# Placing SBUF buffers at multiples of 2048 and 128 bytes in a fused two-block transformer kernel

## The reference, cut to what matters

```python
# first block, for each of 2 layers
h = rmsnorm(x, norm_mix[l])
q, k, v, u, ug, ga, gb = split(h @ w_in[l])
a_out = sliding_window_attention(rope(rmsnorm(q)), rope(rmsnorm(k)), v, sinks[l])
c_out = silu(layernorm(depthwise_conv(u * sigmoid(ug)))) @ w_conv_out[l]
x = x + (sigmoid(ga) * a_out + sigmoid(gb) * c_out) @ w_out[l]
g, up = split(rmsnorm(x, norm_ffn[l]) @ w_gate_up[l])
x = x + (silu(g) * up) @ w_down[l]                    # d_ff = 2816
# second block, 1 layer
mod = silu(c) @ w_ada + b_ada
x = x + g1 * (concat(ssd_mixer(h), stick_breaking_mixer(h)) @ w_out)
x = x + g2 * ((silu(h @ w_gate) * (h @ w_up)) @ w_down)
```

## The kernel before

| buffers | before: byte | rest by 128 | rest by 2048 |
|---|---|---|---|
| x | 16,512 | 0 | 128 |
| hh, hl | 32,896, 49,280 | 0 | 128 |
| raw, wh, wl | 65,664, 73,856, 90,240 | 0 | 128 |
| tmp | 106,624 | 0 | 128 |
| cst | 120,960 | 0 | 128 |
| mh, ah, ssd_h, q, xc | 134,080 | 64 | 960 |
| ml, al, ssd_l | 150,464, 179,136, 158,656 | 64 | 960 |
| oh, ol | 175,040, 191,424 | 64 | 960 |
| square_hi, square_lo, block_sum | 150,464, 154,560, 228,800 | 64 | 960, 960, 1472 |
| ch, glu | 201,664 | 64 | 960 |
| cl, conv | 210,336 | 32 | 1440 |

## Time and profile before

### The profile page before, as it was taken

The page is one execution under the profiler, slowest core; times in us unless marked ns, Lnnn a source line. Parts: engine busy times, 40 slices in busy tenths (PEclk is TensorE's granted clock), DMA queues, the critical chain, the costliest instruction groups (busy, mean ns, idle before and its releaser), DMA issues.

```text
span 2189.6 us, 28930 instructions
## 1 busy us (share of the span) xinstructions
PE 2172.8 (99%) x10369; PEld 1749.6 (80%) x10369; DVE 1195.5 (55%) x1592; ACT 931.8 (43%) x1497; POOL 1060.4 (48%) x527
## 2 busy tenths in 40 slices
PE   9999999999999999999999999999999999999999
PEld 7877778888888887788888888887786678888887
DVE  7877862222436887873222345859877746333301
ACT  5555543222214556544333215336645655444311
POOL 4963334444444883244444443433666753444442
PEclk9999999999999999999999999999999999999999
DMA  5332233333663332232333572322221112333332
GB/s 181 105 92 67 61 95 96 96 96 96 214 209 92 105 101 62 64 92 96 96 96 96 182 238 79 100 84 60 76 87 58 29 49 87 106 96 96 96 96 86
DMA packets 62868, 219.56 MB, mean 100 GB/s; under 512 B 7936, under 2 KB 8192, under 8 KB 62784
## 3 DMA queue, kind: packets, MB, share of 16 engines
q1 hardware_dynamic: 55296, 191.16, 29.0%
q10 hardware_dynamic: 7488, 27.27, 3.7%
HBM read 212.76 MB, written 2.10 MB: 98 GB/s over the span
## 4 chain that ended last, share of the span: by engine, by line
PE 88%; DVE 6%; issue 2%; POOL 2%; ACT 2%; DMA 0%; SPq 0%; ACTq 0%; POOLq 0%
PE bank L1723 27%; PE bank L1725 27%; PE bank L1724 27%; PE bank L1903 1%; POOL soft_lo L497 1%; PE bank L1797 1%; PE bank L1929 1%; PE bank L1963 1%; DVE soft_hi L1616 1%; POOL wl L406 0%; DVE conv L1287 0%; ACT prob L673 0%; PE bank L1937 0%; DMA raw<-stream 0%; DVE conv L1206 0%
## 5 line engine op out<-in xcount | busy, mean ns | idle before, releaser
L406 POOL TENSOR_TENSOR wl<-raw,wh 128x1024 fp32r<-128x1024 f32 x349 | 852.8, 2444 | 1017.8 <-ACT wh L553 1017.7
L1723 PE MATMUL bank<-hh,wh 128*128 128x512 f32 (+1 forms) x1984 | 774.6, 390 | 3.3 <-DVE hl L1425 1.8
L1725 PE MATMUL bank<-hh,wl 128*128 128x512 f32 (+1 forms) x1984 | 765.1, 386 | 0.0
L1724 PE MATMUL bank<-hl,wh 128*128 128x512 f32 (+1 forms) x1984 | 764.5, 385 | 0.0
L553 ACT ACTIVATE wh<-raw 128x1024 fp32r<-128x1024 f32 x351 | 369.9, 1054 | 582.9 <-PE bank L1725 537.6
L1723 PEld LDWEIGHTS bank<-hh,wh 128*128 128x128 f32 x1984 | 373.4, 188 | 81.3 <-issue 3.7
L1725 PEld LDWEIGHTS bank<-hh,wl 128*128 128x128 f32 x1984 | 373.4, 188 | 75.7
L1724 PEld LDWEIGHTS bank<-hl,wh 128*128 128x128 f32 x1984 | 373.7, 188 | 74.5 <-issue 1.7
L1723 PE MATMUL bank<-ah,wh 128*128 (+1 forms) x512 | 201.7, 394 | 0.0
L1725 PE MATMUL bank<-ah,wl 128*128 (+1 forms) x512 | 200.7, 392 | 0.0
L1724 PE MATMUL bank<-al,wh 128*128 (+1 forms) x512 | 198.7, 388 | 0.0
(11 more groups left out here) (377 smaller groups left out, 2734.7 us busy)
## 6 DMA issues: line engine op xcount, KB each, us to landing
raw<-stream SPq DMA_DIRECT2D x351, 512.0 KB, 3.6
ada_w<-ada ACTq DMA_DIRECT2D x48, 512.0 KB, 4.5
x<-x_t ACTq DMA_DIRECT2D x4, 512.0 KB, 7.8
out_t<-x SPq DMA_DIRECT2D x8, 256.0 KB, 2.1
th<-q SPq DMA_DIRECT2D x16, 64.0 KB
th<-q SPq DMA_DIRECT2D x64, 16.0 KB
q<-th SPq DMA_DIRECT2D x16, 64.0 KB, 2.0
cst<-consts SPq DMA_DIRECT2D x1, 640.0 KB, 6.4
```

Of the source, the lines that this page charges most:

```text
L406: nc.gpsimd.tensor_tensor(wl[:, slot, :], raw[:, raw_slot, :], wh[:, slot, :].bitcast(F32), ALU.subtract).then_inc(lo_ready, 1)
L1723: mm(dst, wh[:, slot, w], xh, start=start, stop=False)
L1724: mm(dst, wh[:, slot, w], xl, start=False, stop=False)
L1725: return mm(dst, wl[:, slot, w], xh, start=False, stop=stop)
```

## The change

`cst`, `win_mask`, `mod_gain` and `neg_sink` are declared ahead of `x`. They take 6912 + 1024 + 64 + 64 = 8064 bytes, and so `x` starts at byte 24,576 = 12 x 2048. `sink_exp` and `rden` move into the region of the first stage, behind `k_rstd`. Two paddings of 8 fp32 values (32 bytes) come ahead of `conv` and ahead of `cl`. No instruction is changed, added or moved; only addresses are.

```diff
+        cst = sb("cst", [P, N_CONSTS])
+        win_mask = sb("win_mask", [P, 2 * 2 * P], BF16)
+        mod_gain, neg_sink = sb("mod_gain", [P, 2, KT]), sb("neg_sink", [P, NH])
         x = sb("x", [P, KT, T])
...
-        par, cst = sb("par", [P, N_PARAMS]), sb("cst", [P, N_CONSTS])
-        win_mask, diag_mask = sb("win_mask", [P, 2 * 2 * P], BF16), sb("diag_mask", [P, P], BF16)
+        par = sb("par", [P, N_PARAMS])
+        diag_mask = sb("diag_mask", [P, P], BF16)
...
-        mod_gain = sb("mod_gain", [P, 2, KT])
...
-        neg_sink = sb("neg_sink", [P, NH])
...
-        den, sink_exp, rden = sb("den", [P, 2, 4]), sb("sink_exp", [P, 2, 4]), sb("rden", [P, 2, 4])
+        den = sb("den", [P, 2, 4])
...
             glu = sb("glu", [P, CT, T + TAPS - 1], F32, region)
+            sb("line_up_conv", [P, 8], F32, region)
             conv = sb("conv", [P, CT, T], F32, region)
...
+            sink_exp, rden = sb("sink_exp", [P, 2, 4], F32, region), sb("rden", [P, 2, 4], F32, region)
...
-            sb("pad_glu", [P, CT * (TAPS - 1)], F32, region)
+            sb("pad_glu", [P, CT * (TAPS - 1) + 8], F32, region)
```

## The result

The changed kernel takes 2199.41 us (median of six runs, 2198.89 to 2201.15) beside 2191.08 us of the kernel before (six runs, 2189.64 to 2191.32): 1.0041 times as long, with an interval of 1.003 to 1.0051. It is 8.3 us slower, where 5.7 us of gain were forecast. The profiled execution is at 2199.28 us with a span of 2197.4.

A forecast was written before the change was run, and what follows sets the result against it. The prediction took the spacing of TensorE's matmuls to bound the kernel. Stage buffers gaining 6.0 us, less 0.3 for oh at 256 columns, gave 5.7 us and a forecast median of 2185.4 us, range 2172 to 2199.

The forecast's parts named there:

- What bounds the kernel: Whole kernel: TensorE is busy 2172.8 of 2189.6 us, so its length is set by the spacing of the matmuls.
- Stage buffers reach hh's pace: Products on stage buffers: rest 64 or 32 to 0 brings them to 226.7 ns, 6.0 us gained; chance 0.50.
- The term of ah: Down projections, inputs ah and al: 1536 matmuls go from 228.9 to 226.7 ns, 3.4 us gained.
- that of ssd: Products on ssd_h, ssd_l: 192 matmuls gain 2.2 ns each, 0.4 us, perhaps half as large.
- that of oh: Products on oh, ol: 168 matmuls gain 2.2 ns each, 0.4 us; the 256-column ones lose 0.3 us.
- that of ch: Convolution's output, inputs ch and cl: 192 matmuls go from 232.0 to 226.7 ns, 1.0 us gained.
- hh, hl and the weights move together, so nothing: Low buffers all move by 8064 bytes, distances among them unchanged: zero taken, bounded by 12.6 us lost and 61 us gained.
- oh at 256 columns: Products on oh at 256 columns: 113 ns becomes hh's 120 ns, 48 matmuls lose 7 ns each, 0.3 us.
- Other engines: ScalarE, GpSimd, VectorE: alignment costs them nothing and TensorE covers them; zero, recorded durations within 1%.
- DMA: Transfers are hidden except the first chunk, 7.72 us on the path: between 0 and 0.2 us gained, 0 taken.
- Only the place counts: Rival: slow buffers are slow for lying above byte 131,072, or nothing matters; no change, 2191.1 us, chance 0.20.
- The low buffers get slower: Rival: the 8064-byte shift takes 5712 hh matmuls to ah's pace, 12.6 us lost, 2198.1 us; chance 0.13.

The follow-up runs named there:

- The kernel at rest 64 throughout: Kernel before, with 320 bytes moved ahead of x and 32 bytes ahead of conv and cl, so every input has distance 0 to the weights: 2185.68 us.
- the low part alone: Kernel before, with only x, hh, raw, the weights and tmp moved by 8064 bytes and the stage buffers left in place: 2198.84 us.
- the stage part alone: Kernel before, with only the stage buffers moved (-64 bytes, conv and cl -32), hh and the weights left in place: 2184.55 us.
- the kernel with hh at 64: Kernel with only the stage buffers moved, plus mod's 192 bytes put between hl and raw, so hh and all stage buffers have distance 64: 2202.41 us.

## Why the prediction was wrong, step by step

*What bounds the kernel*: right. Only the spacing of the matmuls moved, and no wait took its place.

*Stage buffers reach hh's pace*: this is the step that failed. It reads the earlier trace rows as three rests by 128 with three spacings. They are as much three distances to the weights, 0, 64 and 32, since wh itself sat at rest 0. The two readings were one in every row of before, and the text separated only rest from place. The kernel at rest 64 throughout (2185.68) shows that the rest is worth nothing, and the low part alone shows that the distance is what counts. The order 0, 64, 32 was read as a ladder; the table has none. The sum of 5.7 us was about right in size for distance 0: the same terms come to 5.1 us in the stage part alone, and that its medians differ by 6.4 is in part the dip of the clock. The term of ah was sized at 3.4 and measured at 3.54, that of mh at 0.8 (0.77), that of ssd at 0.4 (0.18, about the half that was allowed for), that of oh at 0.4 less 0.3 (0.11), and that of ch was oversized, 1.0 for 0.46: its mean before is 231.3 ns and not the 232.0 of ten triples, and it doesn't come to 226.7 ns even at distance 0, but stays at 227.8. In the change as made, the same terms have the opposite sign: 1536 x (233.3 - 228.9) = 6.8 us for ah, 6.9 measured.

*hh, hl and the weights move together, so nothing*: right, and for the reason given. 443 stayed. The sentence held the whole answer and was applied to one side only: nothing was said of the distance between what moves by 8064 and what moves by -64. The table of moves ahead of the prediction has both numbers.

*oh at 256 columns*: 120 ns as forecast, but what sets it isn't the same. Over all its undisturbed matmuls oh is at 113.3 ns before, 118.7 after, and 120.0 at distance 0; and in the kernel with hh at 64, where oh has the distance 64 as well, it is at 117.8 and not at the 113.3 of before. Those two places differ in the distance by 512 (320 before, 64 there), but 320 by itself doesn't give 113.3: hh has it in that same kernel and is at 118.0. What decides is open.

*Other engines*: right. ScalarE writes ah in 633 ns for 632, and GpSimd writes square_lo in 1293 for 1293:
```profile
L770 ACT ACTIVATE ah<-tmp 128x512 f32 x44 | 27.9, 633 | 193.8 <-DVE tmp L1346 193.8
...
L477 POOL TENSOR_TENSOR square_lo<-tmp,square_hi 128x512 fp32r<-128x512 f32 x16 | 20.7, 1293 | 27.9 <-ACT tmp L906 27.9
```
*DMA*: no gain can be told from the runs. The chunk of the earlier trace rows is the second of the stream; ScalarE starts on it at 9.39 us before and at 8.97 after, but in kernels with raw at its old place it did so anywhere from 8.97 to 9.42 (one trace each).

*The rivals.* "Only the place counts" is refuted by the stage buffers at 226.7 ns above 131,072. The note on cachelines in the Trainium skill (SBUF — State Buffer, Specifications) would have the time unchanged; contiguous reads of 512 columns ran at anything from 226.7 to 234.3 ns here, so the measurement decides against it as a rule for TensorE's two streams together. "The low buffers get slower" ended near the measured time, 2198.1, by the wrong route: it named a phase between the reads of the weights and of the moving rows, which is what fits the runs, but looked for it in hh, whose distance cannot change, and not in the stage buffers, whose distance did. Had it been put on the distance, the forecast would still have lacked a price for 128: no row of before has it. With ch and cl (64 and 32) as the nearest, at 232.0 ns, it would have been 2280 x 3.1 ns = 7.1 us lost in the other four inputs, and a forecast of about 2198.

## What to carry to other kernels

When buffers move, write down for each matmul how far its moving rows and its weights move against each other, not only where each ends. Where fp32r products with a fresh weight load each are bound by TensorE, put inputs, low inputs and both weight buffers at the same rest by 256 bytes: here that alone is 5.1 us of 2191 in the stages that lacked it, for buffers moved by 64 bytes, and 16 bytes off costs 5 ns per matmul. If several readings of the rows fit (rest, distance, place), a rival is owed to each of them.

## What the runs showed of the hardware

- The spacing of 512-column fp32r products with a load before each runs from 226.7 to 234.3 ns with the distance between rows and weights by 256 bytes, all at granted clock 1.00. The absolute place of both is free: 2184.55 and 2185.68 us are within the spread of each other.
- 64 is special (228.9 ns), and not symmetric: 192 is at 233.3. The 228.9 is a mean of unequal gaps: in the kernel before, 231.7 ns behind ah·wh, 225.8 behind al·wh and 229.2 behind ah·wl.
- At 256 columns the order is another: oh is at 113.3 ns at the distance 64 (320 by 512), at 117.8 at 64 (64 by 512) and at 192, at 120.0 at 0 and at 118.7 at 128.
- One weight buffer off by 128 slows two of three products of a triple, one moving buffer one of three; both together cost what the first does, 231.1 ns.
- One dip of the granted clock to 0.50 for 3.4 us (1352.5 to 1355.9 us) costs 1.3 us. The same wait of TensorE stands ahead of it in the traces with and without the dip.
